# A hybrid decoder trunk on one core: the state-space part's segment sums from two float32r halves in one buffer

## The reference, cut to what matters

```python
def segsum(a):
    t = a.shape[-1]
    rep = jnp.broadcast_to(a[..., None], a.shape + (t,))
    strict = jnp.tril(jnp.ones((t, t), dtype=bool), -1)
    cs = jnp.cumsum(jnp.where(strict, rep, 0.0), axis=-2)
    return jnp.where(jnp.tril(jnp.ones((t, t), dtype=bool)), cs, -jnp.inf)
...
    adt = (dt * A).reshape(B, c, L, G, HG).transpose(0, 3, 4, 1, 2)
    decay = jnp.exp(segsum(adt))
    cb = jnp.einsum('bclgn,bcsgn->bgcls', Cc, Bc)
    y_diag = jnp.einsum('bghcls,bcsghp->bclghp', cb[:, :, None] * decay, X)
```

## Time and profile before

| | before |
|---|---|
| median of three runs | 2652.9 us (2643.48, 2652.90, 2656.55) |
| the profiled execution, its own time | 2650.03 us |
| its span, first to last instruction | 2647.5 us |
| TensorE matmuls busy | 2556.0 us, 97% of the span |
| VectorE busy | 1581.3 us, 60% |
| ScalarE busy | 1316.9 us, 50% |
| GpSimd busy | 800.3 us, 30% |
| mean granted TensorE clock | 0.985 of full speed |

### The profile page before, as it was taken

One profiled execution on the slowest core, in us unless ns is written; L12 is line 12 of the kernel. 1 busy time (PEld: TensorE's weight loads), 2 busy tenths in 40 slices (PEclk: granted clock), 3 DMA queues, 4 the chain that ended last, 5 costly groups with the idle time before them and its releaser, 6 DMA issues.

```text
span 2647.5 us, 43973 instructions
## 1 busy us (share of the span) xinstructions
PE 2556.0 (97%) x18106; PEld 2352.1 (89%) x18106; DVE 1581.3 (60%) x2547; ACT 1316.9 (50%) x1933; POOL 800.3 (30%) x436
## 2 busy tenths in 40 slices
PE   7999999999899989999999999999999999899999
PEld 7888899899899987878798888989998999888887
DVE  6877567498144545555567775774971445455555
ACT  5486563344444434444544865643444444344444
POOL 0011210088788830000000112101887888300000
PEclk9999999999999999999999999999999999999999
DMA  6532245255544435566545332352554444355555
GB/s 229 190 118 106 81 143 199 96 176 184 167 136 139 140 128 185 196 205 225 187 160 188 115 105 86 130 199 101 184 180 158 143 138 142 127 193 195 193 192 173
DMA packets 95380, 419.26 MB, mean 158 GB/s; under 512 B 10704, under 2 KB 11088, under 8 KB 77776
## 3 DMA queue, kind: packets, MB, share of 16 engines
q1 hardware_dynamic: 95184, 416.46, 46.5%
HBM read 415.37 MB, written 1.05 MB: 157 GB/s over the span
## 4 chain that ended last, share of the span: by engine, by line
PE 88%; DVE 4%; DMA 3%; POOL 2%; ACT 2%; issue 1%; SPq 0%; DVEq 0%; POOLq 0%; ACTq 0%
PE bank L1929 24%; PE bank L349 17%; PE bank L350 17%; PE bank L351 17%; PE bank L1910 4%; DMA xr<-in_xstream 3%; PE bank L702 2%; POOL xr_lo L1641 2%; PE bank L668 1%; PE bank L685 1%; PE bank L706 1%; ACT xr_hi L1636 1%; DVE ring_lo L340 1%; PE bank L1779 1%; PE bank L719 1%
## 5 line engine op out<-in xcount | busy, mean ns | idle before, releaser
L1636 ACT ACTIVATE xr_hi<-xr 128x1024 fp32r<-128x1024 f32 x512 | 541.9, 1060 | 810.8 <-DMA xr<-in_xstream 810.7
L1641 POOL TENSOR_TENSOR xr_lo<-xr,xr_hi 128x1024 fp32r<-128x1024 f32 x256 | 621.3, 2431 | 457.9 <-ACT xr_hi L1636 457.5
L349 PE MATMUL bank<-featH,xr_hi 128*128 128x256 f32 x2048 | 589.8, 288 | 11.0 <-POOL xr_lo L1641 10.9
L350 PE MATMUL bank<-featL,xr_hi 128*128 128x256 f32 x2048 | 578.7, 283 | 0.0
L351 PE MATMUL bank<-featH,xr_lo 128*128 128x256 f32 x2048 | 578.4, 282 | 0.0
L1641 DVE TENSOR_TENSOR xr_lo<-xr,xr_hi 128x1024 fp32r<-128x1024 f32 x256 | 313.5, 1225 | 330.2 <-ACT xr_hi L1636 330.0
L349 PEld LDWEIGHTS bank<-featH,xr_hi 128*128 128x128 f32 x2048 | 389.8, 190 | 12.2 <-issue 9.9
L350 PEld LDWEIGHTS bank<-featL,xr_hi 128*128 128x128 f32 x2048 | 389.7, 190 | 0.0
L351 PEld LDWEIGHTS bank<-featH,xr_lo 128*128 128x128 f32 x2048 | 389.4, 190 | 0.0
L349 PE MATMUL bank<-featH,ring_hi 128*128 128x256 f32 x1216 | 351.4, 289 | 9.2 <-DVE ring_lo L340 6.2
L350 PE MATMUL bank<-featL,ring_hi 128*128 128x256 f32 x1216 | 346.0, 285 | 0.0
(11 more groups left out here) (333 smaller groups left out, 4192.9 us busy)
## 6 DMA issues: line engine op xcount, KB each, us to landing
xr<-in_xstream SPq DMA_DIRECT2D x512, 512.0 KB, 3.3
ring<-in_wstream SPq DMA_DIRECT2D x128, 1024.0 KB, 4.9
first<-in_wstream SPq DMA_DIRECT2D x4, 1024.0 KB, 7.3
smw<-in_small SPq DMA_DIRECT2D x2, 1234.0 KB, 11.4
subk<-in_subkeys SPq DMA_DIRECT2D x2, 1024.0 KB, 8.2
x<-in_x SPq DMA_DIRECT2D x2, 512.0 KB, 6.2
big<-in_mix_row SPq DMA_DIRECT2D x2, 512.0 KB, 5.6
g_row<-in_ffn_row SPq DMA_DIRECT2D x2, 512.0 KB, 3.7
```

What stands on the lines that cost most here:

```text
L349: PE.matmul(o, s_hi_lo[0], m_hi_lo[0], start=first, stop=False)
L350: PE.matmul(o, s_hi_lo[0], m_hi_lo[1], start=False, stop=False)
L1636: A.activation(xr_hi[:, m % XR], xr[:, m % XR], ACT.Copy).then_inc(s_xhi, 1)
L1641: (PO if m < NKEY else V).tensor_tensor(xr_lo[:, m % XR], xr[:, m % XR], xr_hi[:, m % XR].bitcast(F32), ALU.subtract).then_inc(s_xlo_pool ...
```

## The change

The segment sums' matmul is no longer one float32 matmul but two float32r matmuls that add up in the same bank. VectorE splits the small tile `adt` (128x32) once in each layer into `adt_hi` (rounded to float32r) and `adt_lo` (the rest), and copies `strict` once into `strict_r`. GpSimd spreads both halves, so each `adt_upper(n)` is two instructions of 128x512 in place of one. They go to `au_hi` and `au_lo`, which lie where the two buffers of before lay: there is one pair in place of two buffers, and from n = 1 on GpSimd waits for `segsum(n - 1)`.

```diff
+        strict_r = sb("strict_r", [P, P], F32R)
...
+                adt_hi, adt_lo = sb("adt_hi", [P, NT, SH], F32R, mix), sb("adt_lo", [P, NT, SH], F32R, mix)
...
-                    au = xb_flat[:, 0:1024].rearrange("p (b h l) -> p b h l", b=2, h=4)
+                    au = (alias("au_hi", [P, 4, P], F32R, xbcC_at), alias("au_lo", [P, 4, P], F32R, xbcC_at + 4 * 512))
...
-                            PE.matmul(bank[2 + n % 2][:], strict, au[:, n % 2].rearrange("p h l -> p (h l)"),
-                                      start=True, stop=True).then_inc(s_seg, 1)
+                            for a in au:
+                                mm = PE.matmul(bank[2 + n % 2][:], strict_r[:], a[:].rearrange("p h l -> p (h l)"),
+                                               start=a is au[0], stop=a is au[1])
+                            mm.then_inc(s_seg, 1)
...
-                            if n >= 2:
-                                pool.wait_ge(s_seg, past(s_seg) + n - 1)
+                            if n:
+                                pool.wait_ge(s_seg, past(s_seg) + n)
                             else:
                                 pool.wait_ge(s_xt, past(s_xt) + 4)
-                            PO.tensor_tensor(au[:, n % 2], times(upper, 4), over(adt[:, c, 4 * q:4 * q + 4], P),
-                                             ALU.mult).then_inc(s_au, 1)
+                            for a, part in zip(au, (adt_hi, adt_lo)):
+                                ins = PO.tensor_tensor(a[:], times(upper, 4), over(part[:, c, 4 * q:4 * q + 4].bitcast(F32), P),
+                                                       ALU.mult)
+                            ins.then_inc(s_au, 1)
...
+                            dch.add(V.tensor_copy(strict_r[:], strict))
                             dch.add(V.tensor_copy(ptf[:], pt[:]))
...
-                        dch.add(V.scalar_tensor_tensor(adt[:], dt, -1.0, times(expa[:], NT), ALU.mult, ALU.mult))
+                        dch.link(V.scalar_tensor_tensor(adt[:], dt, -1.0, times(expa[:], NT), ALU.mult, ALU.mult))
+                        dch.link(V.tensor_copy(adt_hi[:], adt[:]))
+                        dch.add(V.tensor_tensor(adt_lo[:], adt[:], adt_hi[:].bitcast(F32), ALU.subtract))
```

More of the change, by code:

```diff
@@ L412, in layer_programs @@
                 xbcT = sb("xbcT", [P, FX, S + PAD], F32, early)
+                xbcC_at = -(-nc.sbuf_base // 32) * 32
                 xbcC = sb("xbcC", [P, FX, S], F32, early)
```

## The result

The changed kernel takes 2662.5 us (median of eleven runs, 2655.9 to 2672.1); the kernel before, run beside it, 2650.9 (eleven runs). The ratio is 1.004, 95% interval 1.0029 to 1.0052: slower by 11.6 us in the medians, and under the 0.5% named in the prediction.

What follows compares the result with a forecast made beforehand. TensorE, 88% of the span with hardly a gap in the stage, was taken as the bound. Per layer -3.6 + 1.56 + 5.0 + 2.0 = +4.9, for two +9.8; from 2651 this predicts 2661 us, range 2649 to 2668.

Steps and rivals of the forecast that it cites:

- The matmuls: On TensorE, each `segsum` falls from 0.91 to 0.46 us; eight give 3.6 us gain per layer if nobody waits.
- VectorE's small work: The `strict_r` copy and the `adt_hi` and `adt_lo` instructions fit VectorE's idle time: 0, at most 1.4 us per layer uncovered.
- The spreadings: On GpSimd, each spreading instruction with float32r output takes 1.04 us, with 1.20 kept as upper bound.
- Round 5: TensorE waits 1.56 us ahead of `segsum(5)` for an undisturbed GpSimd pair, with 2.86 us from `segsum(4)`.
- Round 7: TensorE waits 5.0 us ahead of `segsum(7)`: GpSimd's halves wait for `lru_lo` and are torn apart by VectorE's split.
- The clock: TensorE's clock falls behind round 7's wait, costing 2.0 us per layer (0 to 2.35); no fall behind round 5.
- What stands behind: After round 7, VectorE's some 2 us delay is covered by `branch(2)`; the rest shifts with TensorE: no cost.
- A: Rival: pair not torn apart in round 7, which waits 1.56 us, clock stays up; -0.5 per layer, 2650 us; chance 0.17.
- B: Rival: the waits are hidden and the matmuls' gain shows; -7.3 us, 2644 us; chance 0.04.
- C: Rival: round 1 caught too, `segsum(1)` waits 1.4 us; 6.7 per layer, 2664.5 us (2666 with slower spreadings); chance 0.10.
- D: Rival: the clock does not fall behind the waits; 3.0 us per layer, 2657 us; chance 0.12.

Runs made afterwards that it cites:

- e5: Changed kernel with unread matmuls added on TensorE ahead of `segsum(5)` (5) and `segsum(7)` (18); 2659.1 us, ratio 1.0036 to the kernel before.
- e4: Changed kernel with VectorE's `decayed(6)` moved ahead of `lru_lo` and the split; 2653.8 us, ratio 1.0011 to the kernel before.
- e2: Kernel before, float32 and one spreading, with one of its two buffers; 2654.7 us, ratio 1.000.
- e3: Changed kernel with GpSimd spreading the high half alone, read by both matmuls; 2658.2 us, ratio 1.0012 to the kernel before.
- e7: The changed kernel run again unaltered, with a second profile; 2662.7 us, ratio 1.0055 to the kernel before.
- e8: Changed kernel with a second pair of spreading buffers, `decayed(5)` ahead of `gate_branch(0)` and `decayed(7)` ahead of the last split; 2644.2 us, ratio 0.9972 to the kernel before.

## Why the prediction was right

The time was right in sign and size: +9.8 forecast, +9.7 and +10.8 in the stages of two profiles, +11.6 by the medians. The mechanism of the matmuls and of both waits held; that the sum also came so near is in part luck, since round 7 was priced too high and the clock in the first layer too low. The terms per layer, from starts of TensorE's instructions:

| us per layer | forecast | first layer | second layer |
|---|---|---|---|
| eight `segsum` | -3.6 | -3.4 | -3.4 |
| round 5 | +1.56 | +1.53 | +1.54 |
| round 7 | +5.0 | +3.99 | +4.60 |
| clock | +2.0 | +3.3 | +1.5 |
| sum | +4.9 | +5.4 | +4.2 |
| stretch, measured | | +5.37 | +4.34 |

A `segsum` saves 0.40 to 0.45 us (from `segsum(2)` to `segsum(3)` 7.41 before, 6.96 after). The waits are the distances above less 1.35. The clock's term is the length of the low windows times what the clock lacks: 3.4 x (0.47 + 0.49), and 3.4 x 0.44.

- **The matmuls.** Right; 0.2 too large per layer.
- **VectorE's small work.** Right at 0: the idle time behind `kT` took it in.
- **The spreadings.** 1.04 us, not the bound of 1.20.
- **Round 5.** Right to 0.03 us: 2.88 and 2.89 us between the two `segsum` where 2.86 was worked out.
- **Round 7.** The mechanism was right, and in the second layer each of its steps; but that sequence came in one of the four layers profiled (and in both of e5). In the other three the lower clock of round 5 had moved GpSimd to the cheaper meeting with `decayed(6)`, 3.99 to 4.14 us. In the second layer it was 4.60 in place of 5.0, half of that because the low half ended 3.04 us after the high one and not 3.24. That the taking of turns makes the wait is shown by e4, which changes only whom GpSimd meets, and by e2 and e3, which have no second turn (0.9 and 2.5 us).

  The Trainium skill's page Advanced Engine Details and Errata, section VectorE Performance Modes, names only VectorE's two-port modes as what blocks GpSimd, and has none for `tensor_tensor`; the second layer's halves, 2.05 and 3.08 us against 1.04, speak against stopping there. They agree with the Trainium skill's page SBUF — State Buffer, section Who interferes with whom, by which a VectorE instruction with two SBUF inputs contends with GpSimd's reads.
- **The clock.** Its sum was near, 2.4 and 1.4 us by e5 (2.4 in both layers of e7) against the forecast's 2.0, but the step "The 1.56 us of round 5 are far shorter, and I count no fall there" failed. A fall came behind this wait in three of the four layers profiled, though in neither layer of e4, whose instructions up to there are the same. It cost little only because a late `branch(1)` moves GpSimd to a cheaper meeting in round 7: 1.6 us lost, 0.6 won back. e3 missed for the same reason.
- **What stands behind.** Right: from `segsum(7)` to 396 us no row of TensorE has an idle time in brackets, and in the 82 us from 378 us on TensorE is busy for 80.86, against 80.10. It was close: in e4 `decayed(7)` did come late.
- **The rivals.** A fell, since the pair is torn apart in both layers, by the split or by `decayed(6)`. B fell, though e8 shows that its gain was there to be had with another buffer. C did not come, by the 0.21 us that GpSimd was ahead. D fell by the low windows, and e5 is D made by hand: the 3.0 per layer it was given is what e5 shows.

What stays open is why the clock falls behind 1.34 us in one layer and not in the next; no run here varied that alone. Open too are the 3.8 us that e5's median has above its two stages.

## What to carry to other kernels

When one instruction becomes two, count the turns as well as the work: on GpSimd beside a busy VectorE, each of the two can wait for a whole VectorE instruction, so a pair needs the lead that a second buffer gives far more than a single one does. Before a buffer is given up, look where the consumer has least work between two reads (here one `ssd_y`, 1.3 us), for the loss sits there and not in the average round. And behind a new wait of even 1.3 to 2 us on TensorE, count the possible fall of the clock: here one fall cost 1.5 to 1.7 us, as much as the shorter wait itself.

## What the runs showed of the hardware

- The granted clock fell to its lower level, 1.2 GHz, behind waits of 1.34 us (three of the six, with the two of e4), 2.00 (both layers of e3), 3.81, 3.90, 3.95 and 4.40 us: the 3.4 us read behind each show 0.50 to 0.56. It did not fall behind the two waits of 1.78 us in e4. One fall took 1.5 to 1.7 us from TensorE, in one case of e3, where the next 3.4 us were low too (0.63), 3.0.
- Filling such a wait with matmuls that nobody reads keeps the clock at 1.00 and won 1.4 to 2.4 us per layer by the stages (e5).
- GpSimd's 128x512 instruction took 1.04 us undisturbed, 2.05 where it met the rest of a 2.29 us VectorE instruction, and 3.00 to 3.21 where it met a whole one (e3, the changed kernel, e7). VectorE's took 3.12 or 3.13 in place of 2.29 where it waited for one of GpSimd's, whether or not a second one followed (the second layer of the changed kernel, e2, e4).
- One float32 matmul of 128x512 took 0.91 us and two float32r ones 0.46, and in the rounds a `segsum` of two float32r matmuls was 0.40 to 0.45 us quicker, so TensorE does the split form in half the time.
